# Expert weights of a mixture-of-experts stage: three loads of 4 MB per expert in place of six of 2 MB

## The reference, cut to what matters

```python
logits = x @ router_w + router_b                # (320, 32)
top_logit, top_e = lax.top_k(logits, 4)
gate = softmax(top_logit)
# for each expert e, on the tokens that chose it:
h = xblk @ w_gu[e] + b_gu[e]                    # w_gu[e] is 1024 x 2048: 8 MB
hg, hu = split(h, 2)
hg = minimum(hg, 7); hu = clip(hu, -7, 7)
act = (hu + 1) * hg * sigmoid(1.702 * hg)
y = act @ w_down[e] + b_down[e]                 # w_down[e] is 1024 x 1024: 4 MB
x = x + sum over the experts of gate * y
```

## Time and profile before

| | |
|---|---|
| median of 3 runs | 1521.63 us (1521.02 to 1523.74) |
| the profiled execution, its own time | 1521.05 us |
| its span from the first to the last instruction | 1519.0 us |
| mean granted TensorE clock | 0.971 |
| TensorE busy | 1444.5 us, 95% of the span |
| weight load L1014, L1045 matmuls | 450.0 and 226.8 us busy |
| HBM read | 465.08 MB |

### The profile page before, as it was taken

One profiled execution on the slowest core, in us unless ns is written; L12 is line 12 of the kernel. 1 busy time (PEld: TensorE's weight loads), 2 busy tenths in 40 slices (PEclk: granted clock), 3 DMA queues, 4 the chain that ended last, 5 costly groups with the idle time before them and its releaser, 6 DMA issues.

```text
span 1519.0 us, 23798 instructions
## 1 busy us (share of the span) xinstructions
PE 1444.5 (95%) x9323; PEld 695.2 (46%) x9323; DVE 524.0 (34%) x1106; ACT 288.4 (19%) x501; POOL 107.6 (7%) x174
## 2 busy tenths in 40 slices
PE   6977799999999989999999999999999999999995
PEld 4755568866665643333333333333333333333332
DVE  6778664533312142132232222213223122221323
ACT  3111332110314221111111111111111111111111
POOL 1189700000000000000000000000000000000000
PEclk9998889997999989999999999999999999999998
DMA  7953111011667629999999999999999999999991
GB/s 312 180 119 63 56 62 58 31 57 44 272 249 314 241 76 430 427 427 428 428 429 428 428 428 429 428 429 429 428 430 428 428 428 428 429 428 428 428 387 47
DMA packets 42665, 471.60 MB, mean 310 GB/s; under 512 B 4914, under 2 KB 10162, under 8 KB 11124
## 3 DMA queue, kind: packets, MB, share of 16 engines
q1 hardware_dynamic: 36324, 460.88, 72.7%
q10 hardware_dynamic: 6288, 9.95, 3.5%
HBM read 465.08 MB, written 5.74 MB: 310 GB/s over the span
## 4 chain that ended last, share of the span: by engine, by line
PE 82%; DMA 8%; DVE 6%; issue 3%; ACT 1%; DVEq 0%; ACTq 0%; SPq 0%
PE bank L1014 27%; PE bank L1045 13%; PE bank L589 9%; DMA big<-in_w_gu 7%; PE bank L962 5%; PE bank L1064 5%; PE bank L672 2%; PE bank L842 2%; PE bank L977 2%; PE bank L969 1%; PE bank L766 1%; PE bank L1032 1%; PE bank L1023 1%; PE bank L758 1%; PE bank L733 1%
## 5 line engine op out<-in xcount | busy, mean ns | idle before, releaser
L1014 PE MATMUL bank<-big 128*64 128x512 f32 x2048 | 450.0, 597 | 1.0 <-DMA big<-in_w_gu 0.9
L1014 PEld LDWEIGHTS bank<-big 128*64 128x64 f32 x2048 | 144.5, 138 | 292.8 <-issue 287.7
L1857 DVE TENSOR_TENSOR big<-big,bank 128x320 f32<-128x320 f32 x256 | 104.6, 480 | 357.8 <-PE bank L1064 357.8
L1045 PE MATMUL bank<-big 128*64 128x512 f32 x1024 | 226.8, 595 | 0.0
L589 PE MATMUL bank<-big 128*128 128x320 f32 (+1 forms) x688 | 187.4, 431 | 2.3 <-ACT big L1244 1.3
L589 PEld LDWEIGHTS bank<-big 128*128 128x128 f32 x688 | 131.6, 192 | 56.9 <-issue 5.3
L1045 PEld LDWEIGHTS bank<-big 128*64 128x64 f32 x1024 | 70.7, 137 | 131.8 <-issue 127.9
L1843 DVE TENSOR_SCALAR big<-bank 128x512 f32<-128x512 f32 x32 | 22.2, 693 | 310.8 <-PE bank L1014 310.8
L1313 ACT ACTIVATE big<-big 128x512 f32<-128x512 f32 x32 | 20.2, 632 | 504.2 <-DVE big L1843 504.2
L1097 ACT ACTIVATE big<-bank 128x320 f32<-128x320 f32 (+3 forms) x122 | 53.2, 436 | 249.6 <-PE bank L589 58.1
L962 PE MATMUL bank<-big 128*64 128x512 f32 x396 | 94.0, 610 | 0.1
(11 more groups left out here) (357 smaller groups left out, 1238.0 us busy)
## 6 DMA issues: line engine op xcount, KB each, us to landing
big<-in_w_gu SPq DMA_DIRECT2D x128, 2048.0 KB, 16.9
big<-in_w_down SPq DMA_DIRECT2D x64, 2048.0 KB, 16.4
big<-in_dense SPq DMA_DIRECT2D x47, 1024.0 KB, 8.1
big<-u_windows ACTq DMA_DIRECT2D x32, 160.0 KB, 7.5
out_y<-big SPq DMA_DIRECT2D x3, 512.0 KB, 2.7
big<-in_smw SPq DMA_DIRECT2D x1, 1408.0 KB, 19.4
big<-in_xT SPq DMA_DIRECT2D x2, 640.0 KB, 4.6
big<-in_b_gu SPq DMA_DIRECT2D x66, 4.0 KB
```

Source lines behind the costliest of these rows:

```text
L1014: last = mm(ps[bank][part, :], xte[:, k, :], w[:, at:at + 512], start=False, stop=(k == KT - 1))
L1045: last = mm(ps[4][part, :], actT[:, k % 4, (k // 4) * CAP:(k // 4 + 1) * CAP], w[:, k % 4, s * 512:s * 512 + 512], start=(k == 0), stop=(k ...
L1857: tt(part, part, ps[bank][:, 0:T], add).then_inc(psum_free[bank], 1)
```

## The change

The six loads of an expert become three of 4 MB, each into four neighbouring slots. The two of `w_gu` take four consecutive rows (32 KB) to a partition. The one of `w_down` takes both halves of the matrix in one instruction, with two runs of 16 KB to a partition. TensorE waits before k = 0 and k = 4 of the up-projection and before k = 0 of the down-projection. SyncE waits for `load_used` (once per expert now, after k = 3), `psum_full[1]` and `psum_full[4]`. For expert 0 a load waits for the last jobs of four slots. The transposes of the gathered rows step by four columns.

```diff
-LOADS = EXPERT_CHUNKS // 2
-LOAD_SLOT = [EXPERT_SLOT[2 * j] for j in range(LOADS)]
-LOAD_AT = [CHUNK * min(EXPERT_SLOT[2 * j:2 * j + 2]) for j in range(LOADS)]
+LOADS = EXPERT_CHUNKS // 4
+LOAD_SLOT = [EXPERT_SLOT[4 * j] for j in range(LOADS)]
+LOAD_AT = [CHUNK * min(EXPERT_SLOT[4 * j:4 * j + 4]) for j in range(LOADS)]
...
             def load(j, e):
-                src = a["w_gu"][e, j * 2 * P:(j + 1) * 2 * P, :].rearrange("(p i) n -> p (i n)", i=2) if j < 4 else \
-                    a["w_down"][e, (j - 4) * 4 * P:(j - 3) * 4 * P, :].rearrange("(p i) n -> p (i n)", i=4)
-                sp.dma_start(view(LOAD_AT[j], 2 * CHUNK), src).then_inc(ring_full[LOAD_SLOT[j]], 16)
+                if j < 2:
+                    sp.dma_start(view(LOAD_AT[j], 4 * CHUNK), a["w_gu"][e, j * 4 * P:(j + 1) * 4 * P, :].rearrange("(p i) n -> p (i n)", i=4)
+                                 ).then_inc(ring_full[LOAD_SLOT[j]], 16)
+                else:
+                    sp.dma_start(view(LOAD_AT[j], 2, 2 * CHUNK), a["w_down"][e].rearrange("(h p i) n -> p h (i n)", h=2, i=4)
+                                 ).then_inc(ring_full[LOAD_SLOT[j]], 16)
             for j in range(LOADS):
-                for c in range(2):
-                    computed(sp, LAST_JOB[NPRE - EXPERT_CHUNKS + 2 * j + c])
+                for c in range(4):
+                    computed(sp, LAST_JOB[NPRE - EXPERT_CHUNKS + 4 * j + c])
                 load(j, 0)
...
                 for j in range(LOADS):
-                    if j == 3:
+                    if j == 0:
+                        sp.wait_ge(S("load_used"), it)
+                    elif j == 1:
                         sp.wait_ge(psum_full[1], it + BANK_USES[1])
-                    elif j == 5:
+                    else:
                         sp.wait_ge(psum_full[4], it * 2 + (BANK_USES[4] - 1))
-                    else:
-                        sp.wait_ge(S("load_used"), it * 4 + ((j if j < 3 else 3) - 3))
                     load(j, e)
...
             def gathered():
-                pairs = hrow.rearrange("p (j c i) -> p j i c", j=2, i=2)
+                columns = hrow.rearrange("p (c i) -> p i c", i=4)
                 for k in range(4):
-                    last = nc.tensor.transpose(ps[2][:, k * P:(k + 1) * P], pairs[:, k // 2, k % 2], ident)
+                    last = nc.tensor.transpose(ps[2][:, k * P:(k + 1) * P], columns[:, k], ident)
...
                 for k in range(KT):
-                    j = k // 2
-                    if k % 2 == 0:
+                    j = k // 4
+                    if k % 4 == 0:
                         pe.wait_ge(ring_full[LOAD_SLOT[j]], it * 16 + 16 * (USES[LOAD_SLOT[j]] + 1))
-                    w = view(LOAD_AT[j] + k % 2 * CHUNK, CHUNK)
+                    w = view(LOAD_AT[j] + k % 4 * CHUNK, CHUNK)
...
-                    if k % 2 and k < KT - 1:
+                    if k == 3:
                         last.then_inc(S("load_used"), 1)
...
                 for k in range(KT):
-                    j = 4 + k // 4
-                    if k % 4 == 0:
-                        pe.wait_ge(ring_full[LOAD_SLOT[j]], it * 16 + 16 * (USES[LOAD_SLOT[j]] + 1))
-                    w = view(LOAD_AT[j], 4, D)
+                    if k == 0:
+                        pe.wait_ge(ring_full[LOAD_SLOT[2]], it * 16 + 16 * (USES[LOAD_SLOT[2]] + 1))
+                    w = view(LOAD_AT[2] + k // 4 * 2 * CHUNK, 4, D)
```

More of the change, by code:

```diff
@@ L113 @@
 EXPERT_CHUNKS = 12
-LOADS = EXPERT_CHUNKS // 2
-LOAD_SLOT = [EXPERT_SLOT[2 * j] for j in range(LOADS)]
-LOAD_AT = [CHUNK * min(EXPERT_SLOT[2 * j:2 * j + 2]) for j in range(LOADS)]
-assert all(abs(EXPERT_SLOT[2 * j] - EXPERT_SLOT[2 * j + 1]) == 1 for j in range(LOADS))
+LOADS = EXPERT_CHUNKS // 4
+LOAD_SLOT = [EXPERT_SLOT[4 * j] for j in range(LOADS)]
+LOAD_AT = [CHUNK * min(EXPERT_SLOT[4 * j:4 * j + 4]) for j in range(LOADS)]
+assert all(max(EXPERT_SLOT[4 * j:4 * j + 4]) - min(EXPERT_SLOT[4 * j:4 * j + 4]) == 3 for j in range(LOADS))
 class Regions:
@@ L1048, in expert @@
                         last.then_inc(psum_full[4], 1)
-                    elif k == 3:
-                        last.then_inc(S("load_used"), 1)
                 for bank in (0, 1):
```

## The result

| | median | runs |
|---|---|---|
| before | 1521.63 us | 1521.02 to 1523.74 |
| after | 1528.86 us | 1527.23 to 1530.17 |

The ratio is 1.0042, 95% interval 1.0030 to 1.0053: slower by 4.6 to 8.1 us. The profiled execution took 1529.00 us (span 1527.0) against 1521.05 (span 1519.0). The prediction was 1529.2.

A forecast was written before the change was run, and what follows sets the result against it. The prediction took the loads (29.69 us per expert, TensorE 29.18) as the bound; -3.7 + 3.4 + 4.9 + 3.5 = +8.1 on the profiled 1521.05 gave 1529.2 us, range 1524.5 to 1534.

The forecast's parts named there:

- What bounds the kernel: Expert loop: loads take 29.69 us per expert against TensorE's 29.18; one DMA engine carrying the `b_gu` rows sets that period.
- Edit 1: `w_gu` loads in 32 KB runs: period falls from 29.69 to 29.57 us, -3.7 us over 30.67 periods.
- pieces of 16 KB: `w_gu` loads: 32 KB runs are moved in 16 KB pieces and save nothing; +11.8, 1532.9 us; chance 0.15.
- a price per completion: Expert loads: the 7 ns are a load's completion cost, 58 ns a load; three loads fewer save 0.17 per expert, -5.4 us.
- a slower wide pitch: `w_gu` loads: partitions' sources 32 KB apart cost 0.23 us per expert, period 29.92; +18.9, 1540 us; chance 0.08.
- Edit 2: First load for expert 1 needs four slots free, so is issued at 568.11, not 564.69 us: +3.4 us.
- nothing lost, at worst a few tenths: First turns after the later first issue: the load queue does not run empty, with a margin of 0.7 us at expert 2.
- Edit 3: Expert 0's `w_down` as one 4 MB load: `router_b` on the other queue lands 4.9 us later, +4.9 us (bounds 0 to 4.9).
- Edit 4: TensorE waits for four k at once: 7.1 us of up-projection after the last `w_gu` landing, not 3.65: +3.5 us.
- Edit 5: Transposes of gathered rows by four columns take as long as before: 0 us.
- The clock: TensorE's clock at the start, expert 0: full clock -2.7 us or longer half clock about +3; taken as 0, +-3.
- the terms without `router_b`: Whole sum if `router_b` is not delayed: 8.1 - 4.9 = +3.2, 1524.3 us; as a rival, chance 0.11.

The follow-up runs named there:

- no_bias_loads: The kernel after without the loads of `b_gu` for every expert but the first; 1524.25 us, ratio 1.0012 to the kernel before.
- router_first_two_rows: router_first with both `b_gu` rows of an expert in one DMA onto two partitions, not two DMAs; 1521.59 us, ratio 0.9998 to the kernel before.
- gu_16k: The kernel after with two runs of 16 KB to a partition in the `w_gu` loads, not one of 32 KB; 1532.11 us, ratio 1.0067 to before.
- router_first: The kernel after, but SyncE waits for `router_b` to land before issuing expert 0's 4 MB `w_down` load; 1522.72 us, ratio 1.0000 to the kernel before.
- down_only: The kernel before with `w_down` alone in one 4 MB load, `w_gu` still in four of 2 MB; 1529.87 us, ratio 1.0051.
- gu_only: The kernel before with `w_gu` alone in two 4 MB loads, `w_down` still in two of 2 MB; 1523.45 us, ratio 1.0010.

## Why the prediction was right, point by point

**What bounds the kernel: right.** First issue, plus 30.67 turns of the loads, plus what TensorE has left, gives the difference in the ledger above. That one engine with the rows of `b_gu` sets the turn was argued from 29.69 against 29.40 and is shown by no_bias_loads and the landings. The size agrees in the kernel after (0.33 us per expert, two packets of 0.159), but not in router_first_two_rows (0.29 with one packet). So the rows are the cause, but the sum of their packets' times isn't shown to be the price.

**Edit 1, the period: -3.7 predicted, -3.4 in the trace.** 29.56 was measured where 29.57 stood. gu_16k shows that the cause is the one named, a cost of each run whatever its length. Of the alternatives, pieces of 16 KB (no saving), a price per completion and a slower wide pitch, none holds. The near hit is in part luck, though. In the steady stretch (experts 11 to 31) the landings come every 29.55 us against 29.70, which saves about 0.15 us per expert, or some 4.5 over 30.67 turns and not 3.7; about 1 us of it is lost again in the first turns (see edit 2).

The Trainium skill, "DMA: Bandwidth & Descriptors", section "Why small descriptors are slow (HBM only)", names some 3 cycles per packet. At the 850 MHz that the page gives for the fabric, this is an estimate of 3.5 ns a run, which is under half of what was measured: 0.13 us over 16 runs is 8 ns a run.

**Edit 2, the later first issue: +3.4, as read off.** The margin of under a microsecond in the first turns was the thin place of the sum, and "nothing lost, at worst a few tenths" was too kind. The landings from expert 1 to expert 11 come every 29.60 us, where the kernel before has 29.64 there: the saving hardly shows in these ten turns. One landing stands out. The first load of expert 2, issued at 600.35, lands 11.8 us behind the load before it, where later loads take 9.7 to 10.1; the same landing in router_first takes 11.8 too. What held it up, no run isolates. down_only shows what such a gap costs when the margin is gone.

**Edit 3, router_b: +4.9 predicted, +5.2 in the trace,** and router_first takes it all back. It is the one term without which the change would have made no difference. The packets show the mechanism named, queues that take turns, and the landing times fit it: 3.1 us with no load in front, 8.6 beside 2 MB, 13.8 beside 4 MB, 5.5 and 5.2 us for each 2 MB.

**Edit 4, the tail: +3.5 predicted, +3.4.** Edit 5: the four transposes take as long as before.

**The clock:** expert 0 took 15.53 us, 1.0 less than before, and the end of the kernel 1.4 more. Both lie within the 3 us left for it and nearly cancel. At the start the granted clock is at its lower level in a longer idle of TensorE, as the stretches of the kernel after show:

```profile
542.00:547.00 5.00, 0.51 (x3) 0.51 (x3) 3.82 (x21) 4.34 (x7) 0.00 (x0) 0.50 0.00 0
557.00:562.00 5.00, 3.78 (x23) 2.08 (x22) 2.43 (x5) 2.21 (x3) 0.00 (x0) 1.00 0.01 3
562.00:567.00 5.00, 5.00 (x18) 1.48 (x18) 2.85 (x8) 0.00 (x0) 0.00 (x0) 0.66 0.01 3
```

The stretch 542 to 547 is now wholly at 1.2 GHz with TensorE busy for 0.51 of 5 us (4.21 before), and the half-clock stretch that stood at 557 to 562 comes later, in 562 to 567. Expert 0 starts later too, at 562.24 and not 558.20, and has less of it. The 1.4 us at the end all lie behind the last down-projection. Two groups of matmuls there, with the granted clock at 0.55 from 1510 to 1515 us, take 3.67 and 1.70 us where they took 3.32 and 1.26 before; that is 0.8 of it. That the rest is the clock too isn't shown.

**Where the sum flattered itself:** the terms without `router_b` are +3.2, and router_first and gu_only measured 0.0 (-1.4 to 1.4) and +1.5 (0.2 to 2.9). router_first's own ledger has them: 1474.92 - 566.75 = 908.2 for the stream, 4.5 less than before, against +3.4 and +3.4; the rest up to its +1.6 in the span are 1.0 us in the stages before and some tenths of clock. So the period's term is 0.8 larger than predicted there. That the sum of 8.1 came so near to the 7.2 of the medians is partly luck: small errors of both signs met.

## What to carry to other kernels

Here the stream of loads and the engine that eats it were within 2% of each other. In such a case, larger loads are priced by three things that have nothing to do with bandwidth: when the first one may go out, how much work sits behind the last landing, and which small load queues up behind them on another queue. Look for the 16 KB load that someone waits for before enlarging the 4 MB load beside it; here one wait in the issuing program undid the harm. And an average rate hides the slowest DMA engine: compare the turn of the landings with bytes over rate.

## What the runs showed of the hardware that I had not expected

- A run of 32 KB against two of 16 KB saves an engine 8 to 10 ns and no more (29.56 against 29.68 us per 12.58 MB; packets of 1218 against twice 614 ns); the number of loads in which the same runs are issued (three or six) makes no difference beyond 0.01 to 0.02 us per expert.
- Two 4 KB rows per 12.58 MB cost the whole stream 0.33 us, because one of 16 engines carries them and every landing waits for it. At the end of the kernel before it was 10 us behind the first engine and 8 behind the second slowest.
- Rows cut into 256-byte pieces over 16 engines did not remove the lag of one engine but enlarged it (29.55 to 29.66, and 29.69 to 29.85); two rows in one DMA put one row on another engine and left the slowest one's lag where it was. What else holds that engine back stays open.
- Two queues with packets waiting took turns packet by packet, though their packets differed in size (114 of 16 KB against 114 of 4 KB in 6 us), so each small row waited for a large run.
